# Other distances, modulo 512 bytes, between the moving tiles and the weights of the seven products

## What is computed

```
gate, up = jnp.split(h @ w_ffn_in[l], 2, axis=-1)     # 1024 -> 2 x 2816
f = (jax.nn.silu(gate) * up) @ w_ffn_out[l]           # 2816 -> 1024
x = x + _rmsnorm(f, g_post_ffn[l])

def swiglu(x, w1, w2):
    gu = x @ w1
    g, u = gu[..., :D_FF_2], gu[..., D_FF_2:]
    return (jax.nn.silu(g) * u) @ w2
```

## Time and profile before

| | |
|---|---|
| median of 3 executions | 3476.24 us (3472.96 to 3476.84) |
| the profiled execution | 3470.74 us |
| its span, first to last instruction | 3468.9 us |
| PE busy | 3365.4 us, 97% of the span |
| weight loads busy | 2884.7 us, 83% |
| DVE busy | 2462.7 us, 71% |
| ACT busy | 1617.0 us, 47% |
| mean granted clock of TensorE | 0.994 |
| read from memory | 313.84 MB, 91 GB/s |

### The profile page before, as it was taken

How to read it: one execution, slowest core, us unless ns; L and a number is a source line. 1 busy time by engine, 2 the same in 40 slices (tenths; PEclk the granted TensorE clock), 3 DMA queues, 4 the chain that set the end, 5 groups by cost and what they waited for, 6 DMA issues and landing times.

```text
span 3468.9 us, 49474 instructions
## 1 busy us (share of the span) xinstructions
PE 3365.4 (97%) x19557; PEld 2884.7 (83%) x19557; DVE 2462.7 (71%) x3512; ACT 1617.0 (47%) x2387; POOL 55.9 (2%) x84
## 2 busy tenths in 40 slices
PE   7999999999999999999999999999999989999999
PEld 5678988767998799887687899889988767788997
DVE  8669854759882888557895698559864888658863
ACT  4645543455562466326524356425542562335642
POOL 1000000000000000000000000000000000000000
PEclk9999999999999999999999999999999999999999
DMA  4123323212332233232133233323333213322332
GB/s 141 50 73 98 99 97 109 82 49 82 102 114 99 76 113 110 95 104 60 49 91 91 97 98 110 100 94 98 110 104 97 75 44 90 92 97 86 110 104 85
DMA packets 339642, 318.95 MB, mean 92 GB/s; under 512 B 31768, under 2 KB 312164, under 8 KB 339428
## 3 DMA queue, kind: packets, MB, share of 16 engines
q1 hardware_dynamic: 335588, 307.95, 28.0%
q0 software_dynamic: 2048, 6.16, 0.5%
q10 hardware_dynamic: 1792, 1.88, 0.2%
HBM read 313.84 MB, written 2.10 MB: 91 GB/s over the span
## 4 chain that ended last, share of the span: by engine, by line
PE 80%; DVE 15%; ACT 3%; issue 2%; DMA 0%; POOL 0%; DVEq 0%; POOLq 0%
PE products L797 31%; PE products L938 24%; PE products L836 7%; PE small L836 6%; PE small L938 4%; PE products L1199 2%; DVE w_lo L2152 2%; DVE seven_x L2404 1%; PE products L1396 1%; DVE conv L2939 1%; DVE X L2172 1%; DVE x_sums L2393 1%; ACT w_hi L1522 1%; PE small L1273 1%; DVE mla_prob L2599 1%
## 5 line engine op out<-in xcount | busy, mean ns | idle before, releaser
L2152 DVE TENSOR_TENSOR w_lo<-raw,w_hi 128x2048 fp32r<-128x2048 f32 x190 | 435.1, 2290 | 482.7 <-ACT w_hi L1522 482.4
L1522 ACT ACTIVATE w_hi<-raw 128x2048 fp32r<-128x2048 f32 x190 | 363.8, 1915 | 833.1 <-PE products L797 579.8
L797 PE MATMUL products<-a_hi,w_hi 128*128 128x512 f32 (+1 forms) x1216 | 490.8, 404 | 12.8 <-DVE a_lo L2212 10.1
L797 PE MATMUL products<-a_hi,w_lo 128*128 128x512 f32 (+1 forms) x1216 | 477.0, 392 | 0.0
L797 PE MATMUL products<-a_lo,w_hi 128*128 128x512 f32 (+1 forms) x1216 | 476.4, 392 | 0.0
L938 PE MATMUL products<-seven_x,w_hi 128*128 128x256 f32 x2592 | 465.6, 280 | 8.3 <-DVE w_lo L2433 3.2
L938 PEld LDWEIGHTS products<-seven_x,w_hi 128*128 128x128 f32 x2592 | 395.0, 188 | 12.2 <-DVE w_lo L2433 4.4
L938 PE MATMUL products<-seven_x,more_hi 128*128 128x256 f32 x1632 | 375.9, 279 | 3.6 <-ACT rs_b L1631 3.6
L938 PE MATMUL products<-seven_x,w_lo 128*128 128x256 f32 x1296 | 361.6, 279 | 0.0
L797 PEld LDWEIGHTS products<-a_hi,w_hi 128*128 128x128 f32 (+1 forms) x1216 | 229.9, 189 | 70.0 <-issue 16.7
L938 PEld LDWEIGHTS products<-seven_x,more_hi 128*128 128x128 f32 x1632 | 277.7, 188 | 4.8 <-ACT rs_b L1631 4.8
(11 more groups left out here) (463 smaller groups left out, 7228.8 us busy)
## 6 DMA issues: line engine op xcount, KB each, us to landing
raw<-in_ffn_w SPq DMA_DIRECT2D x244, 512.0 KB, 4.1
raw<-in_w_in SPq DMA_DIRECT2D x108, 512.0 KB, 4.6
raw<-in_w_ffn_in SPq DMA_DIRECT2D x88, 512.0 KB, 4.2
raw<-in_w_ffn_out SPq DMA_DIRECT2D x40, 512.0 KB, 4.5
raw<-in_w_out SPq DMA_DIRECT2D x32, 512.0 KB, 4.2
raw<-in_ffn_w SPq DMA_DIRECT2D x24, 384.0 KB, 3.5
raw<-in_w_mem_kv SPq DMA_DIRECT2D x8, 512.0 KB, 4.1
raw<-in_lru_w_out SPq DMA_DIRECT2D x8, 512.0 KB, 3.4
```

What stands on the lines that cost most here:

```text
L797: mm = pe.matmul(G[pair][0:m, into + b, 0:n], w[:, s, at:at + m], x, start=(first or into > 0) and k == 0 and q == 0, stop=(last or ends) ...
L1522: act.activation(w_hi[:, s, :], raw[:, s, :], ACT.Copy).then_inc(hi_ready, 1)
L2152: dve.tensor_tensor(w_lo[:, s, :], raw[:, s, :], w_hi[:, s, :].bitcast(F32), ALU.subtract).then_inc(lo_ready, 1)
```

## The change

It moves tiles in memory; no instruction is added, removed or put in another place in an engine's list. `seven_x` and `late_hi` now begin 16 bytes behind a multiple of 512 (`SHIFT = 16`). `w_hi` and `w_lo` stay at 0, so the distance there is 16. `more_*` and `early_*` go to 480 modulo 512, which makes 16 - 480 = -464, or 48 modulo 512. All other moving tiles and weights stay at 0 modulo 512. The rest of the diff makes room: regions are rounded up to multiples of 512, tiles that stood at a fixed offset of a region get that of a neighbour, and the scratch area for POOL's descriptors shrinks from 8192 to 4096 bytes.

```diff
-ODD = 32
+SHIFT = 16
...
+    def onward(at, residue):
+
+        return -(-(at - residue) // LINE) * LINE + residue
...
+    MORE = onward(REGION_A, 480)
+    MORE_LO = onward(MORE + 10 * KB, 480)
+    LATE = onward(MORE_LO + 10 * KB, 0)
+    top[0] = REGION_B = onward(max(top[0], LATE + 12 * KB + SHIFT), 0)
+    SEVEN = onward(REGION_B, 0)
     h_hi = place("h_hi", [P, FC, SEQ], F32R)
-    top[0] += LINE
-    H_LO = top[0]
+    top[0] = H_LO = onward(max(top[0], SEVEN + 44 * KB + SHIFT), 0)
     h_lo = place("h_lo", [P, FC, SEQ], F32R)
+    EARLY = onward(H_LO + 32 * KB, 480)
+    top[0] = EARLY + 12 * KB
+    top[0] += 2 * LINE
...
-    seven_x = place("seven_x", [P, 11, 4 * HALF], F32R, at=REGION_B + ODD)
-    late_hi = place("late_hi", [P, 3, 4 * HALF], F32R, at=REGION_A + 20 * KB + ODD)
-    more_hi = place("more_hi", [P, 5, QUAD], F32R, at=REGION_A)
-    more_lo = place("more_lo", [P, 5, QUAD], F32R, at=REGION_A + 10 * KB)
-    early_hi = place("early_hi", [P, 3, QUAD], F32R, at=H_LO + 32 * KB)
-    early_lo = place("early_lo", [P, 3, QUAD], F32R, at=H_LO + 38 * KB)
...
-    x_sums = place("x_sums", [P, 11, 4 * HALF], at=REGION_B + ODD)
+    def shifted(name, shape, dt, at):
+
+        n = int(np.prod(shape[1:]))
+        flat = place(name, [P, n + SHIFT // 4], dt, at=at)
+        return flat[:, SHIFT // 4:SHIFT // 4 + n].rearrange("p (c n) -> p c n", c=shape[1])
+
+    seven_x = shifted("seven_x", [P, 11, 4 * HALF], F32R, at=SEVEN)
+    late_hi = shifted("late_hi", [P, 3, 4 * HALF], F32R, at=LATE)
+    more_hi = place("more_hi", [P, 5, QUAD], F32R, at=MORE)
+    more_lo = place("more_lo", [P, 5, QUAD], F32R, at=MORE_LO)
+    early_hi = place("early_hi", [P, 3, QUAD], F32R, at=EARLY)
+    early_lo = place("early_lo", [P, 3, QUAD], F32R, at=EARLY + 6 * KB)
...
+    x_sums = shifted("x_sums", [P, 11, 4 * HALF], F32, at=SEVEN)
...
-    nc = _bacc.Bacc("TRN2", target_bir_lowering=False, num_devices=1, dynamic_dma_scratch_size=8192)
+    nc = _bacc.Bacc("TRN2", target_bir_lowering=False, num_devices=1, dynamic_dma_scratch_size=4096)
```

More of the change, by code:

```diff
@@ L290, in two_blocks @@
     raw = place("raw", [P, 2, UNIT])
-    W_HI = top[0]
+    top[0] = W_HI = onward(top[0], 0)
     w_hi = place("w_hi", [P, 2, UNIT], F32R)
-    W_LO = top[0]
+    top[0] = W_LO = onward(top[0], 0)
     w_lo = place("w_lo", [P, 2, UNIT], F32R)
@@ L298, in two_blocks @@
                 for i, at in enumerate((W_LO + 4 * UNIT, W_HI + 4 * UNIT, BROADCASTS, BROADCASTS + 4 * ROWS_4))]
-    REGION_A = top[0]
+    top[0] = REGION_A = onward(top[0], 0)
     a_hi = place("a_hi", [P, DC, SEQ], F32R)
+    top[0] = A_LO = onward(top[0], 0)
     a_lo = place("a_lo", [P, DC, SEQ], F32R)
     dft = place("dft", [P, TC // 2, 2, SEQ], at=REGION_A)
-    ab = place("ab", [P, TC, SEQ], at=REGION_A + 16 * KB)
+    ab = place("ab", [P, TC, SEQ], at=A_LO)
     rows = place("rows", [P, n_param_tiles, P], at=REGION_A)
     out_tok = place("out_tok", [P, TC, D], at=REGION_A)
-    top[0] += LINE
-    REGION_B = top[0]
+    MORE = onward(REGION_A, 480)
[3 more added lines that the diff above has]
+    SEVEN = onward(REGION_B, 0)
     h_hi = place("h_hi", [P, FC, SEQ], F32R)
-    top[0] += LINE
-    H_LO = top[0]
+    top[0] = H_LO = onward(max(top[0], SEVEN + 44 * KB + SHIFT), 0)
     h_lo = place("h_lo", [P, FC, SEQ], F32R)
+    EARLY = onward(H_LO + 32 * KB, 480)
+    top[0] = EARLY + 12 * KB
+    top[0] += 2 * LINE
     x_tok = place("x_tok", [P, TC, D], at=REGION_B)
@@ L316, in two_blocks @@
     QUAD = 4 * P
-    seven_x = place("seven_x", [P, 11, 4 * HALF], F32R, at=REGION_B + ODD)
-    late_hi = place("late_hi", [P, 3, 4 * HALF], F32R, at=REGION_A + 20 * KB + ODD)
-    more_hi = place("more_hi", [P, 5, QUAD], F32R, at=REGION_A)
-    more_lo = place("more_lo", [P, 5, QUAD], F32R, at=REGION_A + 10 * KB)
-    early_hi = place("early_hi", [P, 3, QUAD], F32R, at=H_LO + 32 * KB)
-    early_lo = place("early_lo", [P, 3, QUAD], F32R, at=H_LO + 38 * KB)
-    more_sums = place("more_sums", [P, 5, QUAD], at=REGION_A + 10 * KB)
-    early_sums = place("early_sums", [P, 3, QUAD], at=H_LO + 38 * KB)
-    x_sums = place("x_sums", [P, 11, 4 * HALF], at=REGION_B + ODD)
+    def shifted(name, shape, dt, at):
[8 more added lines that the diff above has]
+    early_lo = place("early_lo", [P, 3, QUAD], F32R, at=EARLY + 6 * KB)
+    more_sums = place("more_sums", [P, 5, QUAD], at=MORE_LO)
+    early_sums = place("early_sums", [P, 3, QUAD], at=EARLY + 6 * KB)
+    x_sums = shifted("x_sums", [P, 11, 4 * HALF], F32, at=SEVEN)
     h_full = place("h_full", [P, FC, SEQ], at=H_LO)
@@ L404, in two_blocks @@
           for name in ("window", "rot_q", "dup0", "rot_k0", "dup1", "rot_k1", "dft_cos", "dft_sin")}
+    b1[0] = onward(b1[0], 0)
     m_hi = in_b("m_hi", [P, DC, MEM], F32R)
@@ L409, in two_blocks @@
     third_prob = in_b("third_prob", [P, 4, 2 * P])
-    b1[0] = REGION_B
+    b1[0] = YC = onward(REGION_B, 0)
     yc_hi = in_b("yc_hi", [P, LC, SEQ], F32R)
     yc_lo = in_b("yc_lo", [P, LC, SEQ], F32R)
+    b1[0] = onward(b1[0], 0)
+    YA = b1[0]
     ya_hi = in_b("ya_hi", [P, LC, SEQ], F32R)
     ya_lo = in_b("ya_lo", [P, LC, SEQ], F32R)
+    b1[0] = onward(b1[0], 0)
     yb_hi = in_b("yb_hi", [P, LC, SEQ], F32R)
     yb_lo = in_b("yb_lo", [P, LC, SEQ], F32R)
-    REGION_T = b1[0]
+    b1[0] = REGION_T = onward(b1[0], 0)
+    MG_LO = onward(REGION_T + 16 * KB, 0)
     gelu = in_b("gelu", [P, LC, SEQ])
@@ L422, in two_blocks @@
     lru_in = in_b("lru_in", [P, LC, SEQ])
-    glu = place("glu", [P, LC, SEQ], at=REGION_B)
-    conv = place("conv", [P, LC, SEQ], at=REGION_B + 8 * KB)
+    glu = place("glu", [P, LC, SEQ], at=YC)
+    conv = place("conv", [P, LC, SEQ], at=YC + 8 * KB)
     craw_sq = place("craw_sq", [P, 5, SEQ], at=REGION_T)
[L426 to L429, removed]
+    lru_tmp = place("lru_tmp", [P, 3, SEQ], at=YA + 10 * KB)
+    craw = place("craw", [P, 6, SEQ], at=YA + 16 * KB)
+    gate_w = place("gate_w", [P, LC, 2, P], at=YA + 28 * KB)
+    mla_prob.append(place("mla_prob4", [P, ROWS_4], at=YA + 18 * KB))
     mla_prob.append(place("mla_prob5", [P, ROWS_4], at=REGION_T))
@@ L433, in two_blocks @@
     kv_head = place("kv_head", [P, MLA_HEADS, SEQ], at=REGION_T + 16 * KB)
-    v_head = place("v_head", [P, TC, MLA_HEADS * HEAD], at=REGION_T + 32 * KB)
+    v_head = place("v_head", [P, TC, MLA_HEADS * HEAD], at=MG_LO + 16 * KB)
     mg_hi = place("mg_hi", [P, DC, SEQ], F32R, at=REGION_T)
-    mg_lo = place("mg_lo", [P, DC, SEQ], F32R, at=REGION_T + 16 * KB)
-    partial = place("partial", [P, DC, SEQ], at=REGION_T + 16 * KB)
+    mg_lo = place("mg_lo", [P, DC, SEQ], F32R, at=MG_LO)
+    partial = place("partial", [P, DC, SEQ], at=MG_LO)
     def place_of(r):
```

## The result

The changed kernel takes 3483.94 us (median of 19 executions, 3479.90 to 3486.41). The kernel before takes 3474.34 us (19 executions, 3467.43 to 3481.41). The ratio of the two sets of executions is 1.0023, with a 95% interval of 1.0017 to 1.0029; the two medians alone give 1.0028. The change makes the kernel slower, by 8 to 10 us. The prediction said 3449 us, and faster with a chance of 0.50. The measured time lies inside its wide range (3414 to 3498), but on the other side of the time before.

A forecast was written before the change was run, and what follows sets the result against it. PE's time per matmul was taken to bound the kernel; 9072 matmuls at 3.3 ns less gave -30 us, 3 us came back, so 3444 us profiled and 3449 us as median. The range was 3414 to 3498 us.

The forecast's parts named there:

- What bounds the kernel: Six stages of the seven products: PE's time per matmul, 116.7 ns, sets the step of 9.80 us, not waits.
- The parts that were to cost nothing: Writers of the moved tiles, ordinary products at 226.3 ns and the smaller scratch area: nothing taken for any of them.
- value taken: one step of 3.3 ns less on both: Seven products: distances 16 and 48 each save 3.3 ns a matmul, the step seen from 0 to 32; 30 us less.
- the bounds given: Per matmul at 16 and 48: -7.6 ns if all excess goes, +3.3 as at distance 0, +8.8 with the 96 wide excess.
- rival 1: Nothing measurable, 3476 us; a straight line through 0 and 32 gives 118.3 at 16, 115.0 at 48, +2.2 us; chance 0.22.
- Rival 2: Slower: 16 is as good as none, 120.0 ns, 3493 us; with 48 beyond the optimum too, 3506; chance 0.28.
- a constant per weight load: Excess over the columns at distance 0: 13.3 ns with 256 columns, 13.0 with 512, so not per column.
- the 5.5 ns of the 96 wide weights: Matmuls at mixed distances 0 to 384 took 231.8 ns, 5.5 more than at 0; used in the upper bound.
- The share given back: In the stages, a tenth of the 30 us gain, 3 us, taken back for collisions of the denser DVE with PE.
- The rule that spoke against it: Loading weights takes no read bandwidth from the running matmul, so no distance matters: sum zero, 3476 us.

The follow-up runs named there:

- the bursts: Separate kernel without the computation: back-to-back matmuls with weight loads at distances 0 to 512; 256 columns took 120.0 ns at 0, 118.7 at 16, 116.7 at 32, 118.3 at 48.
- at 112: Changed kernel with distance 112 in all 9072 matmuls in place of 16 and 48: 3439.75 us, ratio 0.9899 to the kernel before; measured again, 3445.63 us, 0.9914.
- the kernel with 192: Kernel before with seven_x and late_hi 192 bytes off all weights in place of 32: 3457.28 us, ratio 0.9952.

## Why the prediction was wrong

- **What bounds the kernel** was right. When PE's time per matmul moved, the stages moved with it, within 3 us of 9072 times the difference (11.4 for 11, 27.2 for 30.2).
- **The parts that were to cost nothing** cost nothing: layout and scratch area (1.0000 with distance 32) and writers (1217 ns). The ordinary products kept their rate: the mean from start to start in `by_tokens` was 226.8 ns before (L836) and is 226.9 now (L857), and that of the m tiles 119.6 in both.
- **The step that failed is "value taken: one step of 3.3 ns less on both".** It was a judgement, founded on an argument about where the two reads meet, which no row showed. Measured, 16 is 2.0 ns above 32 and 48 is 1.6 above it in the bursts. In place of -3.3 ns the changed kernel got +1.2 on the average of its products, and in place of -30 us, +11 in the stages. Both distances were inside the bounds given (-7.6 to +8.8), and on the other side. The straight line of rival 1 was near at 16 (118.3 for 118.7) and wrong at 48 (115.0 for 118.3).
- **Rival 2 had the sign and not the reason.** It said that 16 falls back to the 120.0 of distance 0 and gave 3493 to 3506; measured were 118.7 and 3484. It is not nearness to 0 that costs: 96 cost 120.0 in all bursts, as much as 0, and 112, next to it, 113.3.
- **A premise was wrong too:** that a distance has one rate. The rows at 32 already held two patterns of single steps (116, 118, 120, 113 ns in turn in four stages of the kernel before, 116, 117, 117 in two), both with the mean of 116.67. The prediction doesn't speak of them.
- **So was the way from one shape to the other.** The prediction called the excess at distance 0 a constant per weight load, since it was 13 ns with 256 and with 512 columns, and carried the 5.5 ns of the 96 wide weights (512 columns) over to 256 columns as a bound. Away from 0 the two shapes go apart: at 32 the excess over the columns is 10.0 ns with 256 and 20.0 with 512.
- **The share given back** was a tenth, and at 112 a tenth was missing: the matmuls alone are 9072 x 3.33 = 30.2 us shorter and the stages 1088.9 - 1061.7 = 27.2. That the number fits is luck as far as these runs show. The reason given, collisions of a denser DVE with PE, doesn't appear: PE's idle time in the stages is 1088.88 - 1066.35 = 22.5 us before and 1061.67 - 1038.89 = 22.8 at 112. Half of the 3.0 us lies in steps from start to start of over 140 ns, the rest for the most part in the first two steps of a stage, before the rate had settled.
- **The rule that spoke against it** is from the Trainium skill, page "TensorE: Matmul & The Clock Gate", Part 2, "Step-by-step": two independent read ports, so that a weight load takes no read bandwidth from the running matmul. What the prediction drew from it, that no distance matters, doesn't hold here. At a granted clock of 1.00, with one kind of instruction, the distance alone moved a matmul between 113.3 and 123.3 ns. Whether it is read bandwidth that is lost, no run shows.

What is not settled is the mechanism. No run looked at why the distance counts, why it counts modulo 256 bytes, or how a stream falls into one of several rates. Which prelude leads to which state can't be foretold from these runs either.

## What to carry to other kernels

Where matmuls run back to back with a weight load each, the distance between the two tiles modulo 256 bytes is a parameter. With 256 columns of `float32r` the best distance, 112, took 3 to 6% off a matmul against 32 and 0, and 1% off this kernel. It can't be guessed from two neighbouring points, nor from another width: 0 is among the worst with 256 columns and the best with 512. Other types and widths were not measured. A kernel of bursts finds the curve in one run, but only one rate of each distance. Measure each candidate also behind other preludes, and take the one with a single state rather than the one with the best first reading: 112 and 192 had the same rate in the first bursts, and only 112 kept it in the kernel.

## What the runs showed of the hardware

- In bursts with a weight load each, a matmul of 256 columns takes 113.3 to 120.0 ns from start to start over the multiples of 16, the same again 256 bytes further on, and 123.3 at 4 bytes (first run of bursts). At 512 columns distance 0 is among the best (226.7), and others cost up to 7 ns more.
- The same stream has more than one steady rate at nine of the sixteen distances (16: 116.7 and 118.7; 32: 116.7 and 117.8; 192: 113.3 and 117.8). At 16 there is a third, 113.3, seen for one to four products of 12 matmuls in a row. Between bursts at one distance and at different rates only what ran before them differed.
- A stage of 1512 matmuls settled within its first two steps of seven products and then held its state. Executions of the kernel with 192 lay up to 28 us apart; that the states are the cause of that is inferred from one profile.
